# Attention ticks on three engines: outputs taken by VectorE in the same tick, and the value product ahead of the transposes on TensorE

## What is computed

```python
# block 1, twice: 12 heads of 64 in three groups with dilation 1, 4, 16
sc = where(valid, q @ k.T * scale, -inf); p = exp(sc - max); o = (p @ v) / sum(p)
# block 1, twice: 4 heads of 128 over 256 memory tokens
p = softmax(q @ k.T * scale); o = p @ v
# block 2, depth 0: 8 windowed heads of 64 over latent and context keys, with a sink,
# and 4 differential heads: (softmax1 - lam * softmax2) @ v, then an RMS norm per head
# block 2, depth 1: 16 MLA heads, queries and keys of 96, values of 64, 768 keys
p = softmax((q_nope @ k_nope.T + q_rope @ k_rope.T) * scale); o = p @ v
```

## Time and profile before

| | us |
|---|---|
| median of 3 runs | 4615.08 |
| lowest and highest | 4611.87, 4627.31 |
| the profiled execution, its own time | 4629.0 |
| its span, from the first to the last instruction | 4627.2 |

### The profile page before, as it was taken

The page is one execution under the profiler, slowest core; times in us unless marked ns, Lnnn a source line. Parts: engine busy times, 40 slices in busy tenths (PEclk is TensorE's granted clock), DMA queues, the critical chain, the costliest instruction groups (busy, mean ns, idle before and its releaser), DMA issues. The chain is left out here.

```text
span 4627.2 us, 48720 instructions
## 1 busy us (share of the span) xinstructions
PE 4080.3 (88%) x19562; PEld 3323.0 (72%) x19562; DVE 1827.0 (39%) x3076; ACT 1391.6 (30%) x2082; POOL 1419.4 (31%) x644
## 2 busy tenths in 40 slices
PE   6889997999988999799978777789999878879998
PEld 4677765777667776677756666779999657666886
DVE  5343434654634344364344444331111543433113
ACT  3223334323322333332332333231111333343222
POOL 1124542655312354255531000112222100003442
PEclk9899999999989899999988888799999888989999
DMA  2123331444312233244431000012222100002332
GB/s 84 39 61 91 109 90 49 126 131 127 90 43 61 79 110 90 59 123 127 128 86 28 19 19 19 23 41 64 64 60 59 44 14 10 13 20 73 94 93 78
DMA packets 544397, 316.69 MB, mean 68 GB/s; under 512 B 35828, under 2 KB 517167, under 8 KB 544175
## 3 DMA queue, kind: packets, MB, share of 16 engines
q1 hardware_dynamic: 543903, 312.53, 23.1%
q10 hardware_dynamic: 272, 1.05, 0.1%
HBM read 311.44 MB, written 2.10 MB: 68 GB/s over the span
## 5 line engine op out<-in xcount | busy, mean ns | idle before, releaser
L443 POOL TENSOR_TENSOR wlo<-wraw,whi 128x1024 fp32r<-128x1024 f32 (+5 forms) x640 | 1419.2, 2223 | 3172.5 <-ACT whi L436 3171.3
L459 PE MATMUL acc<-hh,whi 128*128 128x512 f32 (+2 forms) x2744 | 1074.4, 392 | 71.0 <-POOL wlo L443 32.3
L461 PE MATMUL acc<-hh,wlo 128*128 128x512 f32 (+2 forms) x2744 | 1043.3, 380 | 0.0
L460 PE MATMUL acc<-hl,whi 128*128 128x512 f32 (+2 forms) x2744 | 1041.7, 380 | 0.0
L436 ACT ACTIVATE whi<-wraw 128x1024 fp32r<-128x1024 f32 (+5 forms) x640 | 624.5, 978 | 882.6 <-DMA wraw<-in_ada_w 273.2
L459 PEld LDWEIGHTS acc<-hh,whi 128*128 128x128 f32 x2744 | 525.2, 191 | 214.3 <-POOL wlo L443 54.2
L460 PEld LDWEIGHTS acc<-hl,whi 128*128 128x128 f32 x2744 | 525.3, 191 | 91.5 <-issue 11.4
L461 PEld LDWEIGHTS acc<-hh,wlo 128*128 128x128 f32 x2744 | 524.4, 191 | 86.2
L999 DVE TENSOR_REDUCE small<-acc 128x1 f32<-128x768 f32 (+1 forms) x160 | 118.7, 742 | 313.5 <-PE acc L796 309.5
L459 PE MATMUL ob<-hh,whi 128*128 128x512 f32 (+2 forms) x576 | 239.1, 415 | 2.0 <-DVEq L764 2.0
L1358 DVE TENSOR_TENSOR t<-acc,sq 128x768 f32<-128x768 f32 (+1 forms) x44 | 36.3, 825 | 499.7 <-PE acc L461 499.7
(11 more groups left out here) (367 smaller groups left out, 6120.1 us busy)
## 6 DMA issues: line engine op xcount, KB each, us to landing
wraw<-in_ffn_w SPq DMA_DIRECT2D x120, 512.0 KB, 3.8
wraw<-in_w_in SPq DMA_DIRECT2D x102, 512.0 KB, 3.8
wraw<-in_ada_w SPq DMA_DIRECT2D x96, 512.0 KB, 4.0
wraw<-in_w_up SPq DMA_DIRECT2D x88, 512.0 KB, 3.9
wraw<-in_w_down SPq DMA_DIRECT2D x32, 512.0 KB, 4.3
wraw<-in_w_out SPq DMA_DIRECT2D x16, 512.0 KB, 4.1
wraw<-in_w_mkv SPq DMA_DIRECT2D x16, 512.0 KB, 3.9
wraw<-in_ab_w_in SPq DMA_DIRECT2D x14, 512.0 KB, 3.8
```

Of the source, the lines that this page charges most:

```text
L443: e.tensor_tensor(wlo[0:rows, s, a:b, 0:w], wraw[0:rows, s, a:b, 0:w], whi[0:rows, s, a:b, 0:w].bitcast(F32), ALU.subtract).then_inc(lo_re ...
L459: e.matmul(o, wh, xh, start=first, stop=False)
L460: e.matmul(o, wh, xl, start=False, stop=False)
L461: return e.matmul(o, wl, xh, start=False, stop=last)
```

## The change

Three things are moved, and no computation, buffer or transfer is added or taken away. On TensorE the product with V of iteration n-1 is issued ahead of the transposes of iteration n in place of behind them. On ScalarE the copy of `pt` for iteration n stands at the end of step n's exponentials and rounding, ahead of the job's `head` and eviction, in place of at the start of step n+1. On VectorE the output of iteration n-1 is taken in step n, behind the maxima, the former job's low half and values, and the combination; before, the output of n-2 was taken there, right behind the maxima. VectorE's loop is one step shorter by that.

```diff
--- before.py
+++ after.py
@@ -855,6 +855,16 @@
                     scores(n + 1)
                 if vt and not (wide and tick):
                     values(vt)
+                if 1 <= n <= N:
+                    t = its[n - 1]
+                    ready(t.get("need_v", t["need"]))
+                    e.wait_ge(s_copied, c.at(s_copied, n))
+                    e.wait_ge(ob_free[0], c.next(ob_free[0]))
+                    slot["pv"] = n
+                    for j, vj in enumerate(t["v"]):
+                        mm = e.matmul(ob[0][:, 0:t["dv"]], sq[:, 0, j * P:j * P + P], vj, start=j == 0,
+                                      stop=j == len(t["v"]) - 1)
+                    mm.then_inc(s_pv, 1)
                 if 0 <= n < N:
                     t = its[n]
                     if len(t["maps"]) == 2:
@@ -871,16 +881,6 @@
                     tr.then_inc(s_tr, 1)
                 if n == N - 1 and N:
                     give(e, acc_free)
-                if 1 <= n <= N:
-                    t = its[n - 1]
-                    ready(t.get("need_v", t["need"]))
-                    e.wait_ge(s_copied, c.at(s_copied, n))
-                    e.wait_ge(ob_free[0], c.next(ob_free[0]))
-                    slot["pv"] = n
-                    for j, vj in enumerate(t["v"]):
-                        mm = e.matmul(ob[0][:, 0:t["dv"]], sq[:, 0, j * P:j * P + P], vj, start=j == 0,
-                                      stop=j == len(t["v"]) - 1)
-                    mm.then_inc(s_pv, 1)
                 if tick:
                     part(tick)
                 if vt and wide and tick:
@@ -921,15 +921,6 @@
             before = None
             for n in range(-1, max(N + 1, len(ticks))):
                 tick = ticks[n + 1] if n + 1 < len(ticks) else None
-                if 1 <= n <= N:
-                    w = len(its[n - 1]["v"]) * P
-                    e.wait_ge(s_tr, c.at(s_tr, n))
-                    if n >= 2:
-                        e.wait_ge(s_pv, c.at(s_pv, n - 1))
-                    e.activation(sq[:, 0, 0:w], ptf[:, 0:w], ACT.Copy).then_inc(s_copied, 1)
-                    if n == N:
-                        e.wait_ge(s_copied, c.next(s_copied, N))
-                        e.sem_inc(pt_free, 1)
                 if n + 1 < N:
                     exps(n + 1)
                     combs += len(its[n + 1]["maps"]) == 2
@@ -939,6 +930,15 @@
                         sums += 1
                         e.wait_ge(s_sum, c.at(s_sum, sums))
                         e.activation(j["hi"], j.get("arrange", same)(j["work"][0:j["span"], 0:j["T"]]), ACT.Copy).then_inc(s_hi, 1)
+                if 0 <= n < N:
+                    w = len(its[n]["v"]) * P
+                    e.wait_ge(s_tr, c.at(s_tr, n + 1))
+                    if n:
+                        e.wait_ge(s_pv, c.at(s_pv, n))
+                    e.activation(sq[:, 0, 0:w], ptf[:, 0:w], ACT.Copy).then_inc(s_copied, 1)
+                    if n == N - 1:
+                        e.wait_ge(s_copied, c.next(s_copied, N))
+                        e.sem_inc(pt_free, 1)
                 if ends(tick):
                     j = jobs[tick[0]]
                     s = c.turn("acc") if wide else None
@@ -1088,13 +1088,11 @@
                     e.sem_inc(s_sum, 1)
 
             before = None
-            for n in range(-1, max(N + 2, len(ticks))):
+            for n in range(-1, max(N + 1, len(ticks))):
                 tick = ticks[n + 1] if n + 1 < len(ticks) else None
                 if n + 1 < N:
                     for m in range(len(its[n + 1]["maps"])):
                         maxima(n + 1, m)
-                if 0 <= n - 2 < N:
-                    result(n - 2)
                 if ends(before):
                     j, s = jobs[before[0]], slots[before[0]]
                     if j["kind"] in ("rope", "pool", "conv2") or j["kind"] == "plain" and j.get("rx"):
@@ -1120,6 +1118,8 @@
                 if n + 1 < N and len(its[n + 1]["maps"]) == 2:
                     combine(n + 1)
                     combs += 1
+                if 1 <= n <= N:
+                    result(n - 1)
                 if ends(tick):
                     j = jobs[tick[0]]
                     s = slots[tick[0]] = c.turn("slab") if wide else None
```

## The result

| | before | after |
|---|---|---|
| median (before: 4 runs, after: 4 runs) | 4621.19 | 4355.88 |
| lowest to highest | 4611.87 to 4627.38 | 4348.56 to 4368.76 |
| span of the profiled execution | 4627.2 | 4352.4 |

The ratio of the runs is 0.943, with a 95% interval of 0.940 to 0.946: 265 us faster. The kernel before has one run more here than in its own table (4627.38 us), so its median stands 6 us higher. The runs are numbered as in their labels: e4 is the fourth.

What follows compares the result with a forecast made beforehand. TensorE, busy 88% of the span, was taken as the bound, held back only by order and waits. Idle time 213 plus clock 75 gave 288 us off: 4341 us, or 4327 on the runs' scale, range 4240 to 4460.

Steps and rivals of the forecast that it cites:

- VectorE's output a step earlier: At the value product: its 242.9 us of waits for VectorE's output go, except where the new place is late itself.
- Idle time: TensorE in the eight attention stretches: 277.7 us of waits less 12, 28 and 25 gives 213 us won.
- the one on ScalarE's eviction: On ScalarE: head and eviction queue behind the copy, but eviction waits for the part's end anyway, so nothing was charged.
- late copies and outputs: Steps with rotary, pooling or convolution work: VectorE's late maxima delay copy and output; 0.55 us for each of 51, 28 us.
- a sign that it would be wrong: On TensorE: the prediction is wrong if scores (L796) begin to wait for exponentials; no size given.
- the ring: Transposes, copy, product, next transposes: 3.5 us a turn, hidden in most steps; 1 us in about 12 steps, 12 us.
- the output behind the combination: Differential steps: the output waits behind two maps' maxima, exponentials and the combination; bare steps leave waits, 25 us.
- The clock: TensorE in the stretches: fewer long waits, fewer falls to 1.2 GHz; 75 us won of a possible 166.
- The clock stays: Rival for the attention stretches: idle time goes but the clock stays as it is; 4402 us, chance 0.25.
- The waits come back elsewhere: Rival: VectorE's late maxima set the pace through exponentials, copy and output; half of 277.7 us returns, 4476 us, chance 0.10.
- The clock falls: Rival on TensorE: product and transposes run at 1.2 GHz in each of 200 iterations; 4688 us, slower, chance 0.04.
- The ring is the bound: Rival: ScalarE's copy stands behind late exponentials every step, so value products wait for it; 4737 us at 2 us, chance 0.02.

Runs made afterwards that it cites:

- e4: VectorE's and TensorE's parts of the change on the kernel before, with ScalarE's order left as before: 4341.76 us, ratio 0.9404.
- e1: Only VectorE's part of the change on the kernel before, TensorE and ScalarE keeping their order: 4350.62 us, ratio 0.9414.
- eleventh run: VectorE's and TensorE's parts, output right behind maxima except in memory attention and MLA's non-rotary steps, ScalarE's MLA key-value eviction ahead of rounding: 4311.64 us, ratio 0.9328 against before.

## Why the prediction was right

The forecast was 4327 us and the measured median is 4356, 29 above it and inside the range of 4240 to 4460 (6 of the 29 are the higher median of before). The likeliest case came: idle time goes, and part of the time at half clock with it. Two of its terms missed in opposite directions, by 55 and 34 us, so it is partly luck that the sum is this near. Step by step:

*VectorE's output a step earlier.* Right, and it is the whole gain: the first run (e1) shows it alone at 0.9414. Of the 242.9 us, 44.7 are left; under 50 were forecast.

*Idle time.* 213 us were forecast to go, 158 went. The five waits that were priced did what was forecast: 277.7 us fell to 62.7, against 64.7 in the sum. What failed is that it put nothing for waits at other lines. There 54 us are new: 27.6 at L806, 17.3 at the scores, 9.3 at L459. For the first, the step that failed is the one on ScalarE's eviction, whose delay was taken to cost nothing, since it waits for the end of the part anyway. In the step behind a rotary job it does not: ScalarE is late, copy and rounding stand ahead of the eviction, and TensorE stands 1.87 us for it (3605.84 to 3607.71). Some 17 of the 28.6 us come with VectorE's part alone (17.9 in the first run) and 10 with the copy's new place. The prediction looked for the late copies and outputs of such steps at L865, at 28 us for all attentions; in MLA that line waits 1.8 us for the copy and never for the output. It also put nothing for the scores, which wait 17.3 us for exponentials, all in the windowed and differential stretch; it had named that as a sign that it would be wrong, and the first run has 10.7 us of it. Against 12 us for the ring, 28 for late copies and outputs and 25 for the output behind the combination stand 18.0 us for the copy (L938), 32.5 for L1015 and 12.2 for L1018: their sum is right, and how it divides was not.

*The clock.* 75 us were taken, from the value of 0.45 us for each at 1.2 GHz. 170 us less are spent there, which is 77. The sum was right and its places wrong, which is luck: in MLA, where nearly all was to go, only 24 of 90 us went, and the dilated stretches, where a third was expected, lost 80 of 139. The clock of both long stretches was to be above 0.92 and is 0.89 and 0.90. MLA was forecast at 305 us and took 329, the windowed and differential one at 350 and took 380; the dilated stretches took 74.2 and 68.2 us for 99.0 and 82.3.

*Not in the sum.* Busy time fell by 111 us, 34 more than the clock gives. In a stream without a break the groups overlap: product and transposes took 1.52 and 0.85 us to their ends, and in an unbroken row above, 1.28 and 0.58 us from start to start. So a break costs about 0.25 us beside the wait itself. The records have 247 breaks of more than 0.03 us in the eight stretches before and 118 after; 129 fewer at 0.25 us are 32 us. This is worked out, not shown by a run of its own.

*The rivals.* "The clock stays" was wrong, by the windows (380 us at 1.2 GHz before, 210 now). "The waits come back elsewhere" came for a quarter of the 213 us: 55 us more than the sum had. "The clock falls" did not come: the order that the change puts in has the higher clock in MLA (0.90, and 0.78 with the transposes first), and a slightly lower one in the windowed and differential stretch (0.89 and 0.91). "The ring is the bound" was wrong: the pair without ScalarE's part, which has it in full, is not slower than the change (14 us less, intervals overlapping). That nothing happens is excluded by the result, and the first run shows that VectorE's output was what held the product.

*The parts.* The prediction gave a value to each of the three. The runs show one that wins everything, one (TensorE's) that costs 168 us alone and wins 9 us beside VectorE's (within the intervals) and 28 beside both, and one (ScalarE's) that costs time wherever it was added: 17 us alone, 33 beside VectorE's, 14 beside both, this last within the intervals. TensorE's and ScalarE's parts without VectorE's were not run.

## What to carry to other kernels

When an engine waits for a buffer to be emptied, look at what stands ahead of the emptying instruction in the list of the engine that does it: here an output that was ready for a whole step stood behind maxima of a later one, and moving that one step of its list gave 270 us of 4621. Of a change in several parts, run each alone: here two of three added nothing to the first, and a version with one of them left out and the output's place chosen for each attention is at 0.933. An order that suits one list of jobs can hurt in another (19 us won and 35 lost by the same edit), so read its effect by stretch and not by the total.

## What the runs showed of the hardware

The granted clock does not follow TensorE's idle time alone. In MLA, 30.8 us idle went with 162 us at 1.2 GHz, 31.3 us with 66, 25.4 us with 9, and in the fourth run 24.1 us with 56; between the first two only the order of transposes and products differs, and in the third 84 wide matmuls stand beside the waits. The order has no fixed sign: the same two kernels have 0.91 with the transposes first and 0.89 with the product first in the windowed and differential stretch. Added work whose result is thrown away made MLA shorter, by 9.4 us over the change and by 18.4 us (319.2 to 300.8) over the eleventh run, the same kernel without it. Each of these figures is from one profiled execution.
